# Norm root moved behind the MLP's products, and squares of the norms added on VectorE

## The reference, cut to what matters

```python
def rmsnorm(t, g, eps=RMS_EPS):
    tf = t.astype(jnp.float32)
    tf = tf * lax.rsqrt(jnp.mean(tf * tf, axis=-1, keepdims=True) + eps)
    return (tf * g.astype(jnp.float32)).astype(t.dtype)

def sq_relu_mlp(h, w1, w2):            # w1: 1024 x 4096, w2: 4096 x 1024
    return jnp.square(jax.nn.relu(h @ w1)) @ w2

# second model, for each of its two layers i
    h = h + rmsnorm(m, g[1])           # m: output of the mixer
    f = sq_relu_mlp(rmsnorm(h, g[2]), mlp_w1[i], mlp_w2[i])
    h = h + rmsnorm(f, g[3])
```

## Time and profile before

| | |
|---|---|
| median of 3 runs | 1748.43 us (1747.85 to 1751.07) |
| the profiled execution's own time | 1749.82 us |
| its span in the trace | 1747.9 us |
| PE busy | 1611.3 us, 92% of the span |
| DVE, ACT busy | 1029.6 us (59%), 746.1 us (43%) |

### The profile page before, as it was taken

One profiled execution on the slowest core, in us unless ns is written; L12 is line 12 of the kernel. 1 busy time (PEld: TensorE's weight loads), 2 busy tenths in 40 slices (PEclk: granted clock), 3 DMA queues, 4 the chain that ended last, 5 costly groups with the idle time before them and its releaser, 6 DMA issues. The chain is left out here.

```text
span 1747.9 us, 33866 instructions
## 1 busy us (share of the span) xinstructions
PE 1611.3 (92%) x14266; PEld 1543.1 (88%) x14266; DVE 1029.6 (59%) x1561; ACT 746.1 (43%) x1034; POOL 61.6 (4%) x82
## 2 busy tenths in 40 slices
PE   3999999989999889999898997999999997799997
PEld 2999989989998879999897995899998985789997
DVE  6999456886655667443676534445335666364443
ACT  2554434872214544443362011456334354456432
POOL 0112000001100001110000000000000000000000
PEclk6999999999999899999999985999999997799999
DMA  9788545442213437544341000244443331235451
GB/s 359 306 337 351 190 146 199 160 145 72 83 44 121 167 123 265 192 163 175 133 144 34 2 2 25 96 169 168 148 174 119 123 121 49 73 121 183 158 188 49
DMA packets 39196, 256.80 MB, mean 147 GB/s; under 512 B 4259, under 2 KB 5668, under 8 KB 9892
## 3 DMA queue, kind: packets, MB, share of 16 engines
q1 hardware_dynamic: 37492, 251.07, 39.6%
q10 hardware_dynamic: 1584, 3.97, 0.6%
HBM read 251.87 MB, written 3.15 MB: 146 GB/s over the span
## 5 line engine op out<-in xcount | busy, mean ns | idle before, releaser
L457 DVE TENSOR_TENSOR w_lo<-raw,w_hi 128x2048 fp32r<-128x2048 f32 (+2 forms) x203 | 456.6, 2249 | 457.6 <-ACT w_hi L449 456.6
L531 PE MATMUL bank<-x_hi,w_hi 128*128 128x256 f32 (+1 forms) x1840 | 535.6, 291 | 36.3 <-DVE x_lo L686 13.5
L449 ACT ACTIVATE w_hi<-raw 128x2048 fp32r<-128x2048 f32 (+2 forms) x203 | 381.5, 1880 | 399.6 <-PE bank L533 366.6
L533 PE MATMUL bank<-x_hi,w_lo 128*128 128x256 f32 (+1 forms) x1840 | 526.9, 286 | 0.0
L532 PE MATMUL bank<-x_lo,w_hi 128*128 128x256 f32 (+1 forms) x1840 | 526.8, 286 | 0.0
L531 PEld LDWEIGHTS bank<-x_hi,w_hi 128*128 128x128 f32 x1840 | 353.0, 192 | 44.9 <-issue 28.4
L533 PEld LDWEIGHTS bank<-x_hi,w_lo 128*128 128x128 f32 x1840 | 353.9, 192 | 0.0
L532 PEld LDWEIGHTS bank<-x_lo,w_hi 128*128 128x128 f32 x1840 | 352.5, 192 | 0.9 <-issue 0.7
L531 PE MATMUL bank<-mh_hi,w_hi 128*128 128x272 f32 (+1 forms) x512 | 147.8, 289 | 6.5 <-PEq L2733 6.5
L533 PE MATMUL bank<-mh_hi,w_lo 128*128 128x272 f32 (+1 forms) x512 | 146.9, 287 | 0.0
L532 PE MATMUL bank<-mh_lo,w_hi 128*128 128x272 f32 (+1 forms) x512 | 146.7, 287 | 0.0
(11 more groups left out here) (523 smaller groups left out, 2566.7 us busy)
## 6 DMA issues: line engine op xcount, KB each, us to landing
raw<-in_stream SPq DMA_DIRECT2D x227, 1024.0 KB, 4.8
raw<-in_stream SPq DMA_DIRECT2D x8, 768.0 KB, 4.2
gate_store<-stage ACTq DMA_DIRECT2D x8, 256.0 KB, 2.0
raw<-in_stream SPq DMA_DIRECT2D x4, 512.0 KB, 3.3
h<-in_h ACTq DMA_DIRECT2D x1, 1088.0 KB, 6.4
zt<-gate_store SPq DMA_DIRECT2D x1, 1024.0 KB, 5.4
gate<-gate_store SPq DMA_DIRECT2D x1, 1024.0 KB, 7.7
out<-h SPq DMA_DIRECT2D x8, 128.0 KB, 1.9
```

The costliest lines, as they stand in the source:

```text
L449: nc.scalar.activation(w_hi[:, s_at % 2, 0:kt], raw[:, r_at % RING, 0:kt], ACT.Copy).then_inc(hi_done, 1)
L457: nc.vector.tensor_tensor(w_lo[:, s_at % 2, 0:kt], raw[:, r_at % RING, 0:kt], w_hi[:, s_at % 2, 0:kt].bitcast(F32), ALU.subtract).then_inc ...
L531: nc.tensor.matmul(out, hi, xh[:, k0 + k, 0:L], start=start, stop=False)
L533: mm = nc.tensor.matmul(out, lo, xh[:, k0 + k, 0:L], start=False, stop=stop)
```

## The change

Three things. **Folding:** for the norms `norm_mix`, `norm_ffn2`, `BothNorms` and those of both mixer outputs and both MLP outputs of the second model, DVE adds the squares of tiles 2, 3 and then 4, 5 onto 0, 1 (`fold`, ahead of the take of pairs 2 and 3), and PE totals four tiles at the end of the section (0, 1, 6, 7) in place of eight along it. `BothNorms` does so for both of its sets. **Late root:** the norms ahead of the two squared-ReLU MLPs become `LateNorm`: x_hi and x_lo are made from h and the gain alone; h is squared in the up block; DVE adds the eight squares in three steps in pairs 13 and 14, PE does one total after pair 14, and the root is made and squared into `rr` beside pair 15. The down banks are taken by DVE, multiplied by `rr`, instead of by ACT's copy. **Dummies:** 72 in the block before (40 + `LATE_BUSY`), none at the start of the up section; ACT splits the up section's second slab in the block before.

```diff
-GAP_BUSY, FIRST_BUSY = 40, 20
+GAP_BUSY, LATE_BUSY, FIRST_BUSY = 40, 32, 20
...
-    add("mlp2_0", 4, by_cols("mlp_w2_2", [8] * 4), [8] * 4, taker="act")
+    add("mlp2_0", 4, by_cols("mlp_w2_2", [8] * 4), [8] * 4)
...
             def total(self, pe, u, sq):
+                if self.folded and u < 3:
+                    return
+                if self.folded:
+                    pe.wait_ge(n_add, self.add0 + 2)
+                    for k in (0, 1):
+                        nc.tensor.matmul(banks[6][:, 0:self.L], const("ones"), sq[:, k], start=k == 0, stop=False)
                 pe.wait_ge(n_sq, 4 * self.q + u + 1)
                 for k in (2 * u, 2 * u + 1):
                     mm = nc.tensor.matmul(banks[6][:, 0:self.L], const("ones"), sq[:, k], start=k == 0, stop=k == DT - 1)
...
+            def fold(self, dve, u, sq):
+                if not self.folded or u not in (2, 3):
+                    return
+                dve.wait_ge(n_sq, 4 * self.q + u)
+                if u == 3:
+                    dve.wait_ge(n_add, self.add0 + 1)
+                pair = sq[:, 2 * u - 2:2 * u]
+                nc.vector.tensor_tensor(sq[:, 0:2], sq[:, 0:2], pair, ALU.add).then_inc(n_add, 1)
...
+        class LateNorm(Norm):
+            def on_act(self, act, mid=None, between=None):
+                for k in range(DT):
+                    nc.scalar.activation(x_hi[:, k, 0:self.L], self.src[:, k], ACT.Identity, bias=0.0, scale=self.a_cols(k)).then_inc(n_hi, 1)
+            def on_dve(self, dve, mid=None):
+                for k in range(DT):
+                    dve.wait_ge(n_hi, self.hi0 + k + 1)
+                    nc.vector.scalar_tensor_tensor(out=x_lo[:, k, 0:self.L], in0=self.src[:, k], scalar=self.a_cols(k),
+                                                   in1=x_hi[:, k, 0:self.L].bitcast(F32), op0=ALU.mult, op1=ALU.subtract).then_inc(n_lo, 1)
...
+            def add_squares(self, dve, sq, n):
+                half = (4, 2, 1)[n]
...
+                nc.vector.tensor_tensor(sq[:, 0:half], sq[:, 0:half], sq[:, half:2 * half], ALU.add).then_inc(n_add, 1)
...
+            def squared_on_dve(self, dve, rr):
+                L = self.L
+                inverse_root(dve, n_y, self.q + 1, stat[:, 0, 0:L], stat[:, 1, 0:L], stat[:, 2, 0:L], stat[:, 3, 0:L], n_ms)
+                link(dve, "dve", nc.vector.tensor_tensor(rr, stat[:, 3, 0:L], stat[:, 3, 0:L], ALU.mult))
...
@@ plain (the down section, and the mixer's output)
-                    if then:
+                    if late_then:
+                        split_hi_ahead(act, order[order.index(sec) + 1])
+                    elif then:
...
+                    def scaled(i, u, U):
+                        norm.fold(dve, u, sq)
+                        outputs_ready(dve, sec, None, u, 0)
+                        for j in range(2):
+                            ins = nc.vector.tensor_tensor(dst[:, 2 * u + j], out_bank(sec, u, j)[:, 0:L], rr, ALU.mult)
+                        ins.then_inc(dve_took, 1)
...
-                        keep_busy(xh[:, 0, 0:P], xh[:, 1, 0:T1], GAP_BUSY)
+                        keep_busy(xh[:, 0, 0:P], xh[:, 1, 0:T1], GAP_BUSY + (LATE_BUSY if late_then else 0))
+                    if then and not late_then:
                         for u in range(4):
                             then.total(pe, u, sq)
...
@@ mlp (the up block)
+                            if i is None and u == 14:
+                                before.root_on_act(act)
-                        before.on_act(act, mid, lambda: split_hi_ahead(act, up))
+                        before.on_act(act)
+                        before.squares(act, squares)
...
-                        pe_pairs(pe, up, x_hi, x_lo, L, norm=before, busy=FIRST_BUSY)
+                        def one_total(i, u, U):
+                            if i is None and u == 14:
+                                before.one_total(pe, squares)
+                        pe_pairs(pe, up, x_hi, x_lo, L, one_total, norm=before)
```

More of the change, by code:

```diff
@@ L212, in make_plan @@
     add("mlp1_1", 16, by_cols("mlp_w1_2", K8, 1), taker="act")
-    add("mlp2_1", 4, by_cols("mlp_w2_2", [8] * 4, 1), [8] * 4, taker="act")
+    add("mlp2_1", 4, by_cols("mlp_w2_2", [8] * 4, 1), [8] * 4)
     return plan, S
@@ L1113, in residual @@
                         def residual(i, u, U):
+                            then.fold(dve, u, sq)
                             outputs_ready(dve, down, i, u, U)
@@ L2000, in total, with fold @@
                         nc.tensor.matmul(banks[5][:, 0:META], const("ones"), self.sq_meta[:, k], start=k == 0, stop=k == DT - 1)
-                pe.wait_ge(n_sq, 4 * self.q + u + 1)
-                for k in (2 * u, 2 * u + 1):
-                    mm = nc.tensor.matmul(banks[6][:, 0:T1], const("ones"), sq[:, k], start=k == 0, stop=k == DT - 1)
+                if u < 3:
+                    return
+                pe.wait_ge(n_add, self.add0 + 4)
+                for k in (0, 1):
+                    nc.tensor.matmul(banks[6][:, 0:T1], const("ones"), sq[:, k], start=k == 0, stop=False)
+                for k in (0, 1):
+                    nc.tensor.matmul(banks[5][:, META:T2], const("ones"), self.sq_both[:, k], start=k == 0, stop=False)
+                pe.wait_ge(n_sq, 4 * self.q + 4)
+                for k in (6, 7):
+                    mm = nc.tensor.matmul(banks[6][:, 0:T1], const("ones"), sq[:, k], start=False, stop=k == DT - 1)
+                mm.then_inc(n_sum, 1)
+                pe.wait_ge(self.n_sq2, 5)
+                for k in (6, 7):
+                    nc.tensor.matmul(banks[5][:, META:T2], const("ones"), self.sq_both[:, k], start=False, stop=k == DT - 1)
+            def fold(self, dve, u, sq):
+                if u not in (2, 3):
+                    return
+                dve.wait_ge(n_sq, 4 * self.q + u)
+                dve.wait_ge(self.n_sq2, u + 1)
                 if u == 3:
[L2005 to L2008, removed]
+                    dve.wait_ge(n_add, self.add0 + 2)
+                for x in (sq, self.sq_both):
+                    nc.vector.tensor_tensor(x[:, 0:2], x[:, 0:2], x[:, 2 * u - 2:2 * u], ALU.add).then_inc(n_add, 1)
             def on_act(self, act, mid, between):
@@ L2654, in build, with plain @@
         rw.close()
-        def plain(sec, xh, xl, dst, before=None, norm=None, then=None, L=T2, store=None):
+        def plain(sec, xh, xl, dst, before=None, norm=None, then=None, L=T2, store=None, rr=None):
+            late_then = isinstance(then, LateNorm)
             with ExitStack() as c, nc.Block() as block:
@@ L2685, in take, with square @@
                             norm.square(act, u, sq)
-                    act_pairs(act, sec, take, ahead=before is not None)
+                    def square(i, u, U):
+                        taken(act, sec, None, u, 0)
+                        norm.square(act, u, sq)
+                    if rr is not None:
+                        act_pairs(act, sec, square)
+                    else:
+                        act_pairs(act, sec, take, ahead=before is not None)
                     if norm:
                         norm.on_act(act)
-                    if then:
+                    if late_then:
+                        split_hi_ahead(act, order[order.index(sec) + 1])
+                    elif then:
                         for u in range(4):
@@ L2697, in _ @@
                         before.on_dve(dve, mid)
-                    dve_pairs(dve, sec, lambda i, u, U: None)
+                    def scaled(i, u, U):
[4 more added lines that the diff above has]
+                        ins.then_inc(dve_took, 1)
+                    if rr is not None:
+                        dve_pairs(dve, sec, scaled)
+                    else:
+                        dve_pairs(dve, sec, lambda i, u, U: norm.fold(dve, u, sq) if norm else None)
                     if norm:
@@ L2715, in mixer_out @@
                 out = sb(f"mixed{tag}", [P, DT, L], c=c)
-                norm, then = Norm(out, L, g_row(layer, 1), add_to=hs), Norm(hs, L, g_row(layer, 2))
+                norm, then = Norm(out, L, g_row(layer, 1), add_to=hs, folded=True), LateNorm(hs, L, g_row(layer, 2))
                 plain(sec, xh, xl, out, norm=norm, then=then, L=L)
@@ L2722, in mlp @@
             out = sb(f"down_out{layer}", [P, DT, L], c=whole)
-            norm = Norm(out, L, g_row(layer, 3), add_to=hs)
+            squares = sb(f"late_sq{layer}", [P, DT, L], c=whole)
+            rr = sb(f"late_rr{layer}", [P, L], c=whole)
+            norm = Norm(out, L, g_row(layer, 3), add_to=hs, folded=True)
             then = make_then()
```

53 lines of the change are left out of this document (40 added, 13 removed).

## The result

The changed kernel takes 1731.76 us (median of 20 runs, 1723.71 to 1750.70) against 1749.96 us for the kernel before, measured beside it (median of 20). The ratio is 0.9898, 95% interval 0.9879 to 0.9917: a gain of 17.8 us, between 14.5 and 21.2. Ratio and interval rest on runs within 1.5% of the fastest of their kernel, so they leave out three runs of the changed kernel above 1750 us and one of the kernel before at 2289.03 us, whose cause isn't known. The forecast was 1727.5 us, a gain of 20.9, in a range of 1723 to 1734: the median lies in the range, 4.3 us above the forecast.

A forecast was written before the change was run, and what follows sets the result against it. PE bounds the kernel (busy 1611 of 1748 us), but a chain across ACT, PE and DVE bounds the seams. 13.2 + 7.0 + 0.1 + 0.3 + 1.6 - 0.9 - 0.4 = 20.9 us gained, so 1727.5 us, range 1723 to 1734.

The forecast's parts named there:

- First seam: Ahead of the second model's first MLP: with the late root, slab 0 of the up products ends 6.6 us sooner.
- Second seam: Ahead of the second model's second MLP: 6.6 us gained, 1.7 of it from a half-clock stretch going away.
- its clock term: At the second seam: 1.7 us of the gain, from a 4 us window at mean clock 0.57 going away.
- The one total: In each second-model up block: one added total costs PE 0.45 us, 0.9 for two; root hidden beside pair 15.
- Folding in the second model: In ev_out, mlp2_0, od_out and mlp2_1: two pairs each lose their totals, 0.86 to 0.90 us per pair, 7.0 gained.
- DVE's takes in place of ACT's: In the last pair of each second-model down product: DVE's bank reads cost 0.2 us more, 0.4 in all.
- Folding in the first model: Net gains of 0.1 us in down1, 0.3 in w_out and 1.6 in down2, after waits and later tails.
- the clock rival: PE's clock falls at the new seams: 1731 us, or 1729 with one fall; chance 0.14.
- lost folds: Rival: w_lo paces PE everywhere, so the second model's 7.0 us of folding stay as waits, 1734.5 us; chance 0.07.

The follow-up runs named there:

- again: The changed kernel itself, run once more for a second profile: 1736.99 us, ratio 0.9918 to the kernel before.
- before_shift: The kernel before with two extra memsets on DVE ahead of the root between the models: 1745.82 us, ratio 0.9978.
- folds_only: The kernel before with every norm folded as in the change, roots left as before: 1750.28 us, ratio 0.9995.
- second_folds: The changed kernel with the first model's three norms (norm_mix, norm_ffn2, BothNorms) not folded: 1725.76 us, ratio 0.9873.
- after_shift: The changed kernel with two extra memsets on DVE ahead of the root between the models: 1724.43 us, ratio 0.9845.
- dummies40: The changed kernel with 40 dummies at each of the two seams instead of 72: 1741.05 us, ratio 0.9947.
- level18: The changed kernel with 18 instead of 12 dummies ahead of each level of the second model's scan: 1727.37 us, ratio 0.9871.
- both_plain: The changed kernel with BothNorms (down2) alone not folded: 1718.83 us, ratio 0.9833; repeated in another set, 1723.99 us, ratio 0.984.

## Why the prediction was right, point by point

The steps are measured on `again` against the kernel before, by distances within a stage, which the slow scan doesn't enter.

**First seam (forecast 6.6).** Timeline of `again`:

```profile
1129.35 8.84 PE L504 MATMUL bank<-x_hi 128*128 128x256 f32 x72
...
1136.78 1.14 DVE L703 TENSOR_TENSOR h<-h,mid 128x272 f32<-128x272 f32 x3
...
1139.68 0.36 PE L531 MATMUL bank<-x_hi,w_hi 128*128 128x272 f32 x1 [1.48 <-DVE x_lo L736]
...
1146.18 1.92 ACT L449 ACTIVATE w_hi<-raw 128x2048 fp32r<-128x2048 f32 x1 [2.10 <-PE bank L533]
```

Set it beside the earlier trace rows. The last add ends at 1136.78 + 1.14 = 1137.92, and the first product starts 1.76 us later, not 6.12. The forecast said 1.2 to 1.4: the 72 dummies end at 1138.19, a little behind DVE (8.84 us against 8.7), and the start is one small hand-over late. From the last add to the end of slab 0 it is 8.26 us against 14.42 (the row of ACT that ends it stands at 1140.96 in the kernel before): a gain of 6.2.

**Second seam (forecast 6.6).** `again`, to be set beside the earlier trace rows:

```profile
1537.61 1.09 DVE L703 TENSOR_TENSOR h<-h,mid 128x256 f32<-128x256 f32 x3
...
1540.91 0.36 PE L531 MATMUL bank<-x_hi,w_hi 128*128 128x256 f32 x1 [1.45 <-DVE x_lo L736]
...
1547.13 1.92 ACT L449 ACTIVATE w_hi<-raw 128x2048 fp32r<-128x2048 f32 x1 [1.99 <-PE bank L533]
```

The first product comes 2.21 us behind the last add (forecast 2.2), the end of slab 0 8.43 us behind it, against 14.82: a gain of 6.4. The half clock of the earlier trace rows is gone here, as forecast (the windows at 1540 show 1.00), but that isn't the change's doing, as the forecast took it. It is gone as well in `before_shift` and `folds_only`, which have the old seam. ACT's row that ends slab 0, and the window at the old seam, in `before_shift`:

```profile
1554.91 1.92 ACT L449 ACTIVATE w_hi<-raw 128x2048 fp32r<-128x2048 f32 x1 [4.17 <-PE bank L533]
...
1548.00:1552.00 4.00, 3.56 (x23) 2.74 (x23) 4.00 (x11) 1.68 (x4) 0.00 (x0) 1.00 0.01 4
```

There the last add ends at 1541.13, and slab 0 13.8 us behind it, against 14.8 in the kernel before. So 1.0 us of the 6.4 (not 1.7) belongs to a stretch that the kernel before has in one execution and not in another, and the late root is worth 5.4 us at this seam, where the forecast without its clock term had 4.9. The sentence of the prediction that the difference between the two old seams may be chance was the right one.

**The one total (forecast -0.9 for two).** From the last pair of the up section to the first w_hi of the down block it takes 1240.68 - 1230.99 = 9.69 us against 1234.93 - 1225.76 = 9.17: 0.52 for the first MLP, where 0.45 was forecast. The gap ahead of the first down product is 3.40 us against 3.33. So the root does fit beside pair 15.

**Folding in the second model (forecast 7.0).** ACT's w_hi starts in `mlp2_0` of `again`:

```profile
1260.70 1.92 ACT L449 ACTIVATE w_hi<-raw 128x2048 fp32r<-128x2048 f32 x1 [4.10 <-PE bank L533]
...
1284.76 1.92 ACT L449 ACTIVATE w_hi<-raw 128x2048 fp32r<-128x2048 f32 x1 [4.10 <-PE bank L533]
...
1308.81 1.92 ACT L449 ACTIVATE w_hi<-raw 128x2048 fp32r<-128x2048 f32 x1 [4.10 <-PE bank L533]
```

and in `od_out`:

```profile
1511.50 1.92 ACT L449 ACTIVATE w_hi<-raw 128x2048 fp32r<-128x2048 f32 x1 [6.52 <-PE bank L533]
1517.13 1.92 ACT L449 ACTIVATE w_hi<-raw 128x2048 fp32r<-128x2048 f32 x1 [2.51 <-PE bank L533]
...
1522.77 1.92 ACT L449 ACTIVATE w_hi<-raw 128x2048 fp32r<-128x2048 f32 x1 [2.51 <-PE bank L533]
```

The pair of `mlp2_0` that took 24.96 in the earlier trace rows takes 24.05 now, and the one of `od_out` that took 6.56 in the earlier trace rows takes 5.64. That is 0.91 and 0.92 per pair, and two pairs each. `od_out` from its first product to the dummies went from 29.11 to 27.31 us (1.80). `mlp2_1` from its first product to the first take of its last bank gained 1.26 where 1.7 was forecast (94.13 and 92.87 us), with one short stretch at half clock more in this execution. `ev_out` can't be read from the pair before and `again`, whose clocks differ there; `second_folds` has 28.72 us for it against 30.72 before, of which 0.2 is lost to half clock ahead of any total: 1.8. DVE's takes in place of ACT's add 0.1 per MLP, not 0.2.

**Folding in the first model (forecast 0.1 + 0.3 + 1.6).** `down1` in `again`, ACT's w_hi starts, to be set beside the first three of the earlier trace rows:

```profile
209.78 1.91 ACT L449 ACTIVATE w_hi<-raw 128x2048 fp32r<-128x2048 f32 x1 [4.14 <-PE bank L533]
...
225.90 1.92 ACT L449 ACTIVATE w_hi<-raw 128x2048 fp32r<-128x2048 f32 x1 [4.21 <-PE bank L533]
```

and its last take on DVE, behind the fold:

```profile
246.18 0.68 DVE L659 TENSOR_TENSOR sq<-sq 128x512 f32<-128x512 f32 x1
246.78 0.87 DVE L1185 SCALAR_TENSOR_TENSOR h<-bank,gain_col,h 128x256 f32<-128x256 f32 x2
```

The pair takes 16.12 us instead of 16.36, and not 15.99: the wait for w_lo takes the total's place, somewhat more than the prediction read it. The last take starts 4.76 us behind its w_hi (242.02) instead of 4.21. The pairs give 0.60, the tail takes 0.54: nothing, as forecast. In `down2` the pairs give 3.0 and the tail takes 1.4, 1.6 in all, as forecast.

`w_out` is the step that was furthest off for its size. DVE's timeline in `again`:

```profile
638.63 0.68 DVE L659 TENSOR_TENSOR sq_f<-sq_f 128x512 f32<-128x512 f32 x1
639.24 0.87 DVE L2036 SCALAR_TENSOR_TENSOR h<-bank,mod,h 128x256 f32<-128x256 f32 x2
640.80 0.69 DVE L659 TENSOR_TENSOR sq_f<-sq_f 128x512 f32<-128x512 f32 x1 [0.69 <-ACT sq_f L635]
641.41 0.87 DVE L2036 SCALAR_TENSOR_TENSOR h<-bank,mod,h 128x256 f32<-128x256 f32 x2
```

The order is the one forecast: the last take stands behind a fold, no longer behind PE as in the earlier trace rows. But the two slabs ahead save 1.30 us, not 0.86, and the tail loses 0.45, not 0.6: 0.85 gained where 0.3 was forecast. It is of no weight in the sum.

**The sum.** 6.2 + 6.4 - 1.0 (two totals, the second taken like the first) - 0.2 (takes) + 1.8 (`mlp2_0`) + 1.8 (`ev_out`) + 1.8 (`od_out`) + 1.3 (`mlp2_1`) + 0.1 (`down1`) + 0.9 (`w_out`) + 1.6 (`down2`) = 20.7 us, against a forecast of 20.9; without the stretch at the second seam, 19.7. So the mechanism and the sizes of the steps were right. The lower group's 21.3 us below before agree with that to less than 1 us only by luck: the scan's 2.9 us are in it as well, if that group scans as `after_shift` does, and short stretches elsewhere differ from profile to profile by as much (one in the first model's mixer costs the first profile of the changed kernel 3.2 us that `again` doesn't lose).

**What the prediction missed, and where it had luck.** The median is 4.3 us above the forecast, outside the 2 us to which it gave a chance of 0.68. It lies near the 1731 of the clock rival, but the fall that makes it isn't at the seams. The range held it because its upper bound was set for falls at the seams and for lost folds, and neither came; with more than half of the runs in the upper group the median would have lain outside. It took everything outside the touched stages as unmoved. Its rule from the Trainium skill ("TensorE: Matmul & The Clock Gate", Part 1: the clock follows how busy PE has lately been, in a phase of its own, so a slow stretch can differ from run to run) was used for the seams alone, where it would have cost 3.4 us. The large effect of that kind was elsewhere: 13 of 30 runs are some 16.4 us slower, and the two that were profiled have a scan 16.5 us longer than before. It is most of the difference between the forecast 1727.5 and the medians of 1731.8 and 1737.0, since the lower group's middle is 1728.7. The rule agrees with the two groups. It doesn't say which kernel has them, and the chance of 0.14 given to a fall of the clock was put on the wrong place.

**What stays open.** The upper group appeared only in kernels with all three of the first model's norms folded (after, `again`, `folds_only`, `dummies40`), apart from one run of `before_shift`; two more kernels with all three folded, `after_shift` (five runs) and `level18` (four), show none. The first model's folds move the scan of the second by a few us and touch nothing in it. The reading that fits all profiles is that what counts is where in the scan the clock falls: at 1.3 to 1.4 us behind its start it stayed low, at 1.5 to 1.7 us it came back. Why a tenth of a us decides between a few us and 65 us of half clock is open, and so is why some kernels meet the bad place in almost half of their runs and others in none. A shift by several different lengths, with the changed kernel beside it on the same chip, would test both and wasn't tried.

## What to carry to other kernels

A positive factor per token can go behind a product and a squared ReLU, and what that frees is the whole chain from the finished tensor to the first product; it should be read as that chain, not as the time of the root. Folding squares on VectorE is worth a total's full time only where PE is the last to finish; in a section paced by the weight split the wait takes its place and the fold lands on the tail. And when runs of a kernel fall into two groups, compare like with like before judging an edit: `folds_only` looks like nothing by its median and is 8 us faster in its lower group. A profile of one group and a median of both don't describe the same thing, and a stage that no edit touched (here the scan, 2.9 us) must be taken out before a total is said to confirm a sum.

## What was not expected of the hardware

PE's clock stayed at half (1.2 GHz) for some 65 us in which the rows have PE busy for 69.66 of 70 us. It began 1.4 us behind an idle of 0.34 us. The kernel before and `both_plain` have the same idle and the same small matmuls (64x32 out of 64x64) there, and have a clock of 0.96 and 1.00 over their 70 us. So a busy share read from the profile doesn't tell whether the clock is granted. The same section of the Trainium skill ties the low clock to an idle PE and the full one to a busy PE; the measurement decides here, and that simple reading doesn't hold for this stretch. The section also warns that the clock's records have been seen to be unreliable. In this case other rows bear them out: 796 matmuls instead of 1116 in the same 70 us, and a scan that is 16.5 us longer than before.

Also, 2 us of added work made no kernel slower: `after_shift` has a median below both medians of the changed kernel. Where the clock's share varies by more than an edit is worth, a small edit is judged by its stage's rows and not by the median.
